# Earlier preparation for a gated recurrence: the output gate in eight own rows, head 0 and gate block 0 inside the first projection, fillers in new places

## The reference

```python
h = rms_norm(x, norm_mix)
proj = h @ w_in       # columns: hq hf hi hog dq dk dv (512 each), gate_hg gate_da (1024 each)
f = lb + (1 - lb) * sigmoid(hf)
o_hg = hgrn2_chunked(hq, 1 - f, hi, log(f))           # 4 heads of 128, chunks of 64 rows
o_hg = rms_norm(o_hg, hg_out_norm) * silu(hog)
# chunk step, b = cumsum(log f) in the chunk, b_ref its middle, b_end its end
scores = tril((q*exp(b-b_ref)) @ (k*exp(b_ref-b)).T)
o      = scores @ v + (q*exp(b)) @ state
state  = exp(b_end)*state + (k*exp(b_end-b)).T @ v
```

## Time and profile before

| what | us |
|---|---|
| runs before | 2768.42, 2768.62, 2769.93 |
| median | 2768.62 |
| profiled execution, span from first to last instruction | 2769.3 |
| PE busy in it | 2656.0 (96%) |

### The profile page before, as it was taken

One profiled execution on the slowest core, in us unless ns is written; L12 is line 12 of the kernel. 1 busy time (PEld: TensorE's weight loads), 2 busy tenths in 40 slices (PEclk: granted clock), 3 DMA queues, 4 the chain that ended last, 5 costly groups with the idle time before them and its releaser, 6 DMA issues. The chain is left out here.

```text
span 2769.3 us, 37102 instructions
## 1 busy us (share of the span) xinstructions
PE 2656.0 (96%) x13666; PEld 2212.2 (80%) x13666; DVE 1844.9 (67%) x2490; ACT 1308.2 (47%) x1917; POOL 384.0 (14%) x343
## 2 busy tenths in 40 slices
PE   8999999898899899999999999989999999999999
PEld 7887777777788888888888888778888778888887
DVE  5870175457443588888888667756634885867978
ACT  3111143566532277787777421255543552535353
POOL 0222111200121122222222012110010000000000
PEclk9999999999999899999999999999999999999999
DMA  3114223310443399999999432000031625253451
GB/s 127 51 50 133 73 73 115 127 54 16 147 163 138 110 364 373 389 384 376 373 371 366 173 107 60 15 1 1 1 130 46 243 76 213 91 193 142 152 182 61
DMA packets 140825, 433.63 MB, mean 157 GB/s; under 512 B 23313, under 2 KB 45585, under 8 KB 108945
## 3 DMA queue, kind: packets, MB, share of 16 engines
q1 hardware_dynamic: 123584, 398.20, 40.0%
q0 software_dynamic: 10656, 20.99, 2.1%
q10 hardware_dynamic: 6448, 12.58, 1.3%
HBM read 385.58 MB, written 63.96 MB: 162 GB/s over the span
## 5 line engine op out<-in xcount | busy, mean ns | idle before, releaser
L2384 DVE TENSOR_TENSOR w_lo<-w_raw,w_hi 128x2048 fp32r<-128x2048 f32 x192 | 437.1, 2293 | 65.2 <-ACT w_hi L2318 60.3
L2318 ACT ACTIVATE w_hi<-w_raw 128x2048 fp32r<-128x2048 f32 x187 | 355.8, 1925 | 39.4 <-PE banks L2443 39.4
L3219 PE MATMUL banks<-b_parts,a_parts 128*128 128x512 f32 x1344 | 307.0, 390 | 6.2 <-DVE a_parts L3274 6.2
L3219 PE MATMUL banks<-a_parts,b_parts 128*128 128x512 f32 x1344 | 306.0, 389 | 2.3 <-DVE a_parts L3274 1.2
L3219 PEld LDWEIGHTS banks<-b_parts,a_parts 128*128 128x128 f32 x1344 | 251.8, 188 | 60.9 <-DVE a_parts L3274 8.7
L3219 PEld LDWEIGHTS banks<-a_parts,b_parts 128*128 128x128 f32 x1344 | 252.0, 188 | 55.2 <-DVE a_parts L3274 1.6
L3248 ACT ACTIVATE b_parts<-w_quarter 128x1024 fp32r<-128x1024 f32 x112 | 118.5, 1058 | 281.7 <-PE banks L3219 267.0
L634 POOL TENSOR_TENSOR w_lo<-w_raw,w_hi 128x512 fp32r<-128x512 f32 (+2 forms) x128 | 148.3, 1164 | 714.8 <-ACT w_hi L613 713.8
L613 ACT ACTIVATE w_hi<-w_raw 128x512 fp32r<-128x512 f32 (+2 forms) x128 | 70.8, 565 | 364.5 <-PE banks L686 346.7
L3268 DVE TENSOR_TENSOR b_parts<-w_quarter,b_parts 128x1024 fp32r<-128x1024 f32 x112 | 136.8, 1221 | 132.6 <-ACT b_parts L3248 132.6
L686 PE MATMUL banks<-w_hi,act_hi 128*128 128x512 f32 (+1 forms) x576 | 219.1, 380 | 5.4 <-POOL w_lo L634 3.1
(11 more groups left out here) (512 smaller groups left out, 5567.1 us busy)
## 6 DMA issues: line engine op xcount, KB each, us to landing
w_raw<-in_w SPq DMA_DIRECT2D x192, 1024.0 KB, 7.5
a_parts<-scratch_x_parts SPq DMA_DIRECT2D x42, 1024.0 KB, 4.8
w_raw<-in_w_in SPq DMA_DIRECT2D x72, 256.0 KB, 2.7
w_quarter<-in_w_up SPq DMA_DIRECT2D x16, 1024.0 KB, 6.9
w_quarter<-in_w_down SPq DMA_DIRECT2D x16, 1024.0 KB, 7.4
scratch_x_parts<-a_parts SPq DMA_DIRECT2D x14, 1024.0 KB, 5.1
scratch_gateT<-gate_staged SPq DMA_DIRECT2D x32, 256.0 KB, 2.1
gate<-scratch_gateT SPq DMA_DIRECT2D x32, 256.0 KB, 3.3
```

The costliest lines, as they stand in the source:

```text
L2318: act.activation(hi[c % SLOTS][:, :], raw[c % TILES][:, :], ACT.Copy).then_inc(hi_done, 1)
L2384: dve.tensor_tensor(lo[c % SLOTS][:, :], raw[c % TILES][:, :], hi[c % SLOTS][:, :].bitcast(F32), ALU.subtract).then_inc(lo_done, 1)
L3219: mm = pe.matmul(out, left, right, start=(start and n == 0), stop=(stop and n == 2))
```

## The change

1. `stage` is replaced by `hog_rows`, eight rows of one bank each in dq's place. SiLU evictions don't wait for stores any more; there is a wait for dq's store in front and one store per four rows. The store of dk moves from tile 40 to tile 31, and ACT's waits for stores at the end of the stage go; each store has its own semaphore.
2. A class `HgrnOperands` takes the preparation of a head out of `hgrn_stage`; for head 0, and the lower bounds, it runs inside the first projection. SP loads the constants behind tile 30, after waits for the end of dk's rotation and for dv's store. DVE does the bounds, `decays(0)`, `sums(0)` ahead of the hq copies and `operands(0)` between the hq and the hi copies. ACT does the exponential of the bounds and the logarithm behind tile 40 and the four exponentials behind tile 41.
3. Gate block 0 has high and low parts of its own; its load moves from the last tile to tile 52, its `high` and `low` to the end of ACT's and POOL's programs in this stage. Blocks 1 and 2 need no wait for a buffer.
4. Fillers: none ahead of head 0; 6 between the two halves of the transposes; 14, 16 before the sums; 14 (12 for heads 1 to 3) and 14 before the outputs; 74 are left behind head 3.
5. ACT's order in the recurrence is new; `gates.low(8)` moves from the attention stage to the end of the recurrence on POOL, ahead of the stores of `o_hg`.

```diff
     def hog_to_dram(act):
-        for b in range(8):
-            act.wait_ge(ready, 8 * index["hog"] + b + 1)
-            if b >= SLOTS:
-                act.wait_ge(stored[b % SLOTS], 16 * (b // SLOTS))
-            act.activation(stage[:, b % SLOTS, :], v.bank[b][:, :], ACT.Silu).then_inc(free, 1)
-            act.wait_ge(free, 8 * index["hog"] + b + 1)
-            act.dma_start(d["hog"][b * P:(b + 1) * P, :], stage[:, b % SLOTS, :]).then_inc(stored[b % SLOTS], 16)
+        act.wait_ge(dq_kept, 16)
+        n = 8 * index["hog"]
+        for half in range(2):
+            for b in range(4 * half, 4 * half + 4):
+                act.wait_ge(ready, n + b + 1)
+                act.activation(hog_rows[:, b, :], v.bank[b][:, :], ACT.Silu).then_inc(free, 1)
+            t = slice(4 * half, 4 * half + 4)
+            act.wait_ge(free, n + 4 * half + 4)
+            act.dma_start(rows_of(d["hog"])[:, t, :], hog_rows[:, t, :]).then_inc(hog_kept, 16)
...
+    def first_constants(sp):
+        sp.wait_ge(turned_in, 2 * NT)
+        sp.wait_ge(dv_kept, 16)
+        hg.load(sp)
...
-    after(index["hq"], 0, keep_keys)
+    after(index["hf"], 7, keep_keys)
+    after(index["hq"], 0, hg.bound_exp)
+    after(index["hq"], 0, lambda act: hg.log(act, 0))
+    after(index["hq"], 1, lambda act: hg.exponentials(act, 0))
     def act_after(act):
-        act.wait_ge(kept, 48)
-        for i in range(SLOTS):
-            act.wait_ge(stored[i], 16 * (8 // SLOTS))
+        v.gates.high(act, 0)
+    def pool_after(pool):
+        v.gates.low(pool, 0)
...
         norm("dk", k_heads, 1, NT)
+        hg.lower_bounds(dve, then)
+        dve.wait_ge(free, 8 * index["hf"] + 8)
+        dve.wait_ge(dk_kept, 16)
+        hg.decays(dve, then, 0)
+        dve.wait_ge(hog_kept, 32)
+        hg.sums(dve, then, 0)
         copy("hq", lambda b: v.hqT[:, b % 4, (b // 4) * N:(b // 4) * N + N])
+        dve.wait_ge(free, 8 * index["hq"] + 8)
+        hg.operands(dve, then, 0)
         copy("hi", lambda b: v.hv[:, b, :])
...
-    FILL = [(84, 10, 16, 10, 12)] + 3 * [(20, 10, 16, 10, 12)]
+    FILL = [(0, 6, 14, 16, 14, 14)] + 3 * [(20, 6, 14, 16, 12, 14)]
...
                 for half in range(2):
+                    if half:
+                        fill(FILL[h][1])
                     if h or half:
                         pe.wait_ge(rows_done, 2 * h + half)
```

More of the change, by code:

```diff
@@ L553, in turn, with dense_stage @@
             mm.then_inc(self.turned, 1)
-def dense_stage(v, tiles, dve_program, act_steps=None, act_after=None, sp_before=None, sp_steps=None, sems=None, prelude=None, tail=None, ring=None, head=None):
+def dense_stage(v, tiles, dve_program, act_steps=None, act_after=None, sp_before=None, sp_steps=None, sems=None, prelude=None, tail=None, ring=None, head=None, pool_after=None):
     nc, sem = v.nc, v.sem
@@ L884, in project1_stage @@
     rot = at("rot", temps + 6, [P, 4, 256])
-    SLOTS = 2
-    stage = at("stage", temps + 10, [P, SLOTS, N])
+    hog_rows = at("hog_rows", FREE + 48, [P, NT, N])
     cos, sin = at("cos", 29, [P, NT, DA_D // 2]), at("sin", 30, [P, NT, DA_D // 2])
@@ L890, in project1_stage @@
     tables, link = sem("tables"), sem("dve_link")
-    staged, stored = sem("hog_staged"), [sem(f"hog_stored{i}") for i in range(SLOTS)]
-    turned_in, kept = sem("rope_done"), sem("rows_kept")
+    turned_in, dv_kept, dq_kept, dk_kept, hog_kept = sem("rope_done"), sem("dv_kept"), sem("dq_kept"), sem("dk_kept"), sem("hog_kept")
     v.gates = GateColumns(v)
+    v.hg = hg = HgrnOperands(v)
     def load_tables(sp):
@@ L1006, in hgrn_stage @@
     o = FREE + 48
-    k_rel, q_rel, k_end, k_ = (at(n, o + kb, [P, S]) for n, kb in (("k_rel", 0), ("q_rel", 4), ("k_end", 16), ("k_in", 20)))
-    q_dec = [at(f"q_dec{i}", o + 8 + 4 * i, [P, S]) for i in range(2)]
-    b_ = at("b", o + 24, [P, S])
+    hg = v.hg
+    k_rel, q_rel, k_end, q_dec, dec, causal = hg.k_rel, hg.q_rel, hg.k_end, hg.q_dec, hg.dec, hg.causal
     k_rows = at("k_rows", o + 28, [P, NT, P])
@@ L1012, in hgrn_stage @@
     st = at("state", o + 36, [P, NCH, P])
-    keep = at("keep", o + 44, [P, S])
     small = o + 48
[L1015 to L1018, removed]
     ssum, root, inv, itmp = (at(f"o_{n}", small + 0.75 + 0.125 * i, [P, HG_H, NT]) for i, n in enumerate(("ssum", "root", "inv", "tmp")))
-    raw_first_free = small + 2
-    consts, link, lb_exp, sig = sem("consts"), sem("dve_link"), sem("lb_exp"), sem("sig")
-    f_done, ln_done, to_exp, exps, ops = sem("f_done"), sem("ln_done"), sem("to_exp"), sem("exps"), sem("operands")
+    link, ops = sem("dve_link"), hg.ops
     scores, scT_done, tr_done, rows_done = sem("scores"), sem("scT_done"), sem("tr_done"), sem("rows_done")
@@ L1048, in _ @@
             gates.load(sp, 1)
[L1049 to L1052, removed]
             for b in range(HG_BLOCKS):
@@ L1062, in _ @@
         def _(act):
[L1063 to L1075, removed]
             def rows(h):
@@ L1149, in _ @@
             pool.memset(scT[:, :, :, :], 0.0).then_inc(zero, 1)
-            gates.low(pool, 0)
             gates.low(pool, 1)
@@ L1157, in _ @@
             gates.low(pool, 7)
+            gates.low(pool, 8)
             for h in range(HG_H):
@@ L1246, in norms @@
                     dve.tensor_tensor(x, x, inv[:, h, :].unsqueeze(2).broadcast_to([P, NT, HG_D]), ALU.mult).then_inc(normed, 1)
-            lower_bounds()
-            decays(0)
-            sums(0)
-            operands(0)
-            decays(1)
+            hg.decays(dve, then, 1)
             causal_scores(0)
             states(0, 0)
-            sums(1)
+            hg.sums(dve, then, 1)
             states(0, 1)
-            operands(1)
-            decays(2)
+            hg.operands(dve, then, 1)
+            hg.decays(dve, then, 2)
             causal_scores(1)
@@ L1263, in _ @@
             states(1, 0)
-            sums(2)
+            hg.sums(dve, then, 2)
             states(1, 1)
-            operands(2)
-            decays(3)
+            hg.operands(dve, then, 2)
+            hg.decays(dve, then, 3)
             causal_scores(2)
@@ L1271, in _ @@
             states(2, 0)
-            sums(3)
+            hg.sums(dve, then, 3)
             states(2, 1)
-            operands(3)
+            hg.operands(dve, then, 3)
             causal_scores(3)
@@ L1321, in _ @@
                 for half in range(2):
-                    fill(FILL[h][1 + half])
+                    fill(FILL[h][2 + half])
                     n = 2 * h + half
@@ L1332, in _ @@
                 for half in range(2):
-                    fill(FILL[h][3 + half])
+                    fill(FILL[h][4 + half])
                     if h:
@@ L1530, in _ @@
                     pool.wait_ge(q_zero, 2 * i + a + 1)
-            for b in range(HG_BLOCKS, GATE_BLOCKS):
+            for b in range(HG_BLOCKS + 1, GATE_BLOCKS):
                 gates.low(pool, b)
```

165 lines of the change are left out of this document (102 added, 63 removed).

## The result

The changed kernel takes 2753.12 us in the median of five runs (2752.23 to 2756.54), the kernel before 2768.42 (five runs): ratio 0.9942, 95% interval 0.9930 to 0.9953, 15.3 us shorter. Forecast were 2751.4 and a range of 2747 to 2757.

What follows compares the result with a forecast made beforehand. PE, 96% busy, was taken as the bound, losing time at four places. The terms -6.7 - 3.5 - 6.6 - 0.4 = -17.2 took 2769.3 to 2752.1, less 0.7 for the profiled span: 2751.4 us, range 2747 to 2757.

Steps and rivals of the forecast that it cites:

- hog_rows, -6.7: Projection, hog to hq: evictions no longer wait for stores, so hq's whole loss of 6.7 us goes.
- The wait for dq's store: Projection, ahead of hog's evictions: the new wait ends in time, store in by about 236 at the latest, costing nothing.
- The waits on SP: Projection, SP's queue before tile 31's load: waiting for dv's store delays PE by nothing, with 16 us of room; cost 0.
- the chain ahead of the hq copies: Projection, head 0's preparation on DVE and ACT: 11.7 us, done at 285.7, 3.0 us to spare; cost 0, bounds 0 and +3.
- rival A: Head 0's preparation comes too late for the hq copies; six us of delay give +3, 2754.5 us; chance 0.11.
- The stage's start, -3.5: Projection to recurrence: PE starts 1.45 us behind its last matmul, not 4.95, since head 0 is already prepared.
- rival C: Recurrence's start: small scores and transposes don't bring the clock back, head 0 runs at 1.2 GHz, 2777 us; chance 0.03.
- the 2.37 us of head 0: Recurrence before the change: PE's wait for ACT's bank 0 copy, full speed behind it, taken as sign the clock holds.
- The recurrence, -6.6: Recurrence: new filler order and shorter waits give 133.0 us against 139.6; head 0 25.9, heads 1 to 3 30.1 each.
- the wait for bank 0: Recurrence, heads 1 to 3: PE's 0.69 us wait for ACT's copy goes, a switch of shapes adds 0.15.
- POOL's stores at T + 131; PE ends at T + 133: Recurrence's end, T being its start: POOL's stores end at T + 131, before PE, so nothing is late.
- Attention's start, -0.4: Attention's start: first scores 2.0 us earlier, 1.6 eaten by slow clock behind PE's 3.4 us stand; bounds 0 and -3.6.

Runs made afterwards that it cites:

- e3: Changed kernel, but hog's SiLU evictions go through two rows again, each waiting for the store two before: median 2759.5 us.
- e10: Kernel before plus hog's rows and gate block 0 prepared in the projection, head 0 still prepared in the recurrence: median 2765.0 us, ratio 0.9982.
- e4: Changed kernel, but the 6 fillers between the two halves of the transposes go to the next place: median 2759.5 us.
- e1: Changed kernel, but on POOL gate block 8's low part stands behind the output stores of heads 0 to 2, ahead of head 3's only: median 2753.1 us.
- e2: Changed kernel, but the four stores of the recurrence's output go out on SP's queue instead of POOL's: median 2750.7 us.
- the second execution: The changed kernel measured and profiled again, unaltered: median 2753.5 us.
- e9: Changed kernel, but gate block 0's high and low parts are made at the recurrence's start again, its load staying early: median 2755.5 us.
- e5: Changed kernel, but 28 instead of 16 fillers ahead of the attention's first scores, 17 instead of 20 in each of the first four units: median 2752.9 us.

## Why the prediction was right, and where not

*hog_rows, -6.7.* Right, 6.71 measured, and e3 gives 6.7 back. The wait for dq's store, for which I gave up to 14 us of room, cost nothing.

*The waits on SP, the chain ahead of the hq copies, 0.* Right for PE. The chain ended at 284.5 against 285.7, by two errors of opposite sign: from `decays` to the scan it took 2.7 us (276.20 to 278.94) where 4.7 was put, and the scan with its subtractions 5.6 where 4.7 was put, one of them being slow beside POOL, as rival A had it. The table load costs 1.3 us to the activation behind it (273.85 to 275.15), not the 2.66 of the Trainium skill's page "ScalarE: Activation LUTs", section "What ACT_TABLE_LOAD costs".

*The stage's start, -3.5.* Right, 4.95 became 1.45. The clock did not fall there, and rival C with its transposes didn't come: the granted clock is 1.00 from 334 to 364 us. The stand here was 1.45 us; the argument from the 2.37 us of head 0, behind which the next matmuls ran at full speed, was weaker than it looked, for in e10 the clock fell behind a wait of 2.4 us at the same place (0.61).

*The recurrence, -6.6.* Measured -8.2. The mechanism was right; heads 1 to 3 take 29.8 us each and not 30.1, head 0 25.4 and not 25.9. The term that was mis-sized is the wait for bank 0, "- 0.69 + 0.15" per head, 0.54 net. e4 has 0.9 per head, and so have the periods: 27.50 + 14 x 0.2267 = 30.7 without the term, 29.8 measured. I took the idle time from the bracket where the distance of the starts counts, the very thing that the prediction's first paragraph says of the busy share.

*"At the end ... POOL's stores at T + 131; PE ends at T + 133."* This is the step that failed. T + 131 was the time to issue them; they were issued even sooner, at T + 128.4. But the last of them lands at 469.7, 8.1 us after it went out, and the stage waits for that: +2.7 us, shown by e1 and e2. I had costed the moved subtraction on POOL's and PE's queues and not the DMAs behind it. The trace of before shows no such wait, only the room: POOL's last store went out at 478.82 and landed at 483.3, 3.0 us before the next stage began at 486.28. Held back by the subtraction, the first three went out right ahead of the last one, which then took 8.1 us to land, where it took 4.5 before and 3.9 in e1.

*Attention's start, -0.4.* The scores come 1.95 us sooner behind the start (2.0 forecast), PE stands 2.55 us ahead of them (3.4), and the clock fell behind the stand as forecast. That last part was half luck: in the second execution it didn't. From the stage's start to filler 600 it comes out at -0.2 and -1.8 in the two profiles.

The sum: -6.7 - 3.5 - 8.2 + 2.7 - 0.2 = -15.9, as in the spans (forecast -17.2). Two errors of 1.6 and 2.7 us with opposite signs, so 2753.1 came closer to 2751.4 than the steps deserve. Of the rivals, none cost PE anything; the hold-up beside POOL that A counts on came once, 0.9 us, within its room of 3 us.

## What to carry to other kernels

Whoever moves work ahead of DMA issues on an engine has to follow the DMAs to their landing and ask whether the engine's end of stage waits for it; moving the issues to another queue can be worth as much as the move itself. The early gate block was worth 2.3 us beside the early head 0 (e9) and next to nothing without it (e10): ask what PE meets next when the first wait is gone. Size a wait by the distance between starts, not by the idle time in the list of waits, and read positions in the trace against a common origin when effects are a few us: they resolved 0.1 us here as long as the clock didn't fall, the medians 2 to 3.

## What the runs showed of the hardware

POOL's end of a stage waited for the landing of its own stores: next stage at 470.3 with four stores of 512 KB issued one behind the other from 458.9 to 462.4, which landed some 2 us apart, the last at 469.7; at 467.6 with three of them issued by 447, the last landing at 465.0 (e1). Stores of the same bytes from SP's queue held nothing up: the last landed at 468.3, 0.4 us behind the next stage's start at 467.9 (e2). Two executions of the same program had the clock's slow stretch at different places around the same stand of PE (0.86 then 0.58 in one, 0.68 then 1.00 in the other), worth 1.6 us; and the same work behind filler 600 took between 2207.3 and 2214.2 us. These times go mostly with the granted clock of that stretch in the trace, 0.987 on the mean in e2 (2207.3) and 0.983 in e3 and e4 (2214.2 and 2213.9), 0.984 to 0.987 in the others. So do the runs of the kernel before beside e5, from 2763.7 us at 0.987 to 2773.6 at 0.983. Why the clock is granted differently no run here shows.
